# Folding the routing weight and 1+g2 into the experts' eviction, and rewriting the last phase of a two-layer decoder trunk

## The reference

```
expert, weight = top-1 group, top-2 experts in it        # per token: 2 experts, 2 weights
xbuf[dest]     = t[tok]                                  # tokens sorted by expert, 128 to a block
ybuf           = (silu(xbuf @ w_gate[e]) * (xbuf @ w_up[e])) @ w_down[e]
out[tok]      += ybuf[dest] * weight                     # two rows for each token
x              = layer_norm(ALPHA * x + (1 + g2) * out)
```

## Time and profile before

| | us |
|---|---|
| median of three runs (4647.74 to 4658.24) | 4656.67 |
| the profiled execution, its own time | 4658.7 |
| its span, first to last instruction | 4656.5 |
| route, layer 0: up to the store of the block table | 1312.3 |
| experts, layer 0: about | 1315 to 2032 |
| project("k") with Combine | 2032.6 to about 2414 |
| experts, layer 1: last store issued | 4466.4 |
| last phase, first issue to last instruction | 4470.1 to 4656.5 |

### The profile page before, as it was taken

One profiled execution on the slowest core, in us unless ns is written; L12 is line 12 of the kernel. 1 busy time (PEld: TensorE's weight loads), 2 busy tenths in 40 slices (PEclk: granted clock), 3 DMA queues, 4 the chain that ended last, 5 costly groups with the idle time before them and its releaser, 6 DMA issues. The chain is left out here.

```text
span 4656.5 us, 54505 instructions
## 1 busy us (share of the span) xinstructions
PE 3894.4 (84%) x17372; PEld 2848.0 (61%) x17372; DVE 2109.5 (45%) x4726; ACT 1530.3 (33%) x2925; POOL 686.2 (15%) x560
## 2 busy tenths in 40 slices
PE   6999795969779999958979979979957679999930
PEld 1788574858645555537767758868846545555510
DVE  5000215844445545546644332234349655455546
ACT  1222203623223333333321122245635323333322
POOL 0111000211100110114420003300013111011124
PEclk8999897979779999979989989989978679999965
DMA  8322312543179999965546532244444279999964
GB/s 290 113 94 77 122 60 88 180 147 105 65 250 382 383 383 381 383 228 170 177 130 200 170 118 78 65 128 127 148 145 137 71 271 382 383 382 383 382 215 176
DMA packets 637597, 950.82 MB, mean 204 GB/s; under 512 B 42309, under 2 KB 499925, under 8 KB 616213
## 3 DMA queue, kind: packets, MB, share of 16 engines
q1 hardware_dynamic: 587790, 775.23, 49.5%
q0 software_dynamic: 27360, 99.63, 5.8%
q10 hardware_dynamic: 22328, 74.48, 4.0%
HBM read 746.62 MB, written 202.62 MB: 204 GB/s over the span
## 5 line engine op out<-in xcount | busy, mean ns | idle before, releaser
L1416 PE MATMUL ex_gu<-ex_wgu,ex_hT 128*128 128x512 f32 x2016 | 918.3, 598 | 17.9 <-DMA ex_wgu<-in_moe_w_up_dram 10.9
L1416 PEld LDWEIGHTS ex_gu<-ex_wgu,ex_hT 128*128 128x128 f32 x2016 | 369.3, 191 | 416.4 <-issue 403.2
L1537 DVE TENSOR_TENSOR ex_wds<-ex_wd,ex_wds 128x2048 fp32r<-128x2048 f32 x126 | 288.8, 2292 | 251.8 <-ACT ex_wds L1476 251.8
L1435 PE MATMUL ex_acc<-ex_wds,ex_aT 128*128 128x512 f32 x1512 | 382.8, 402 | 6.1 <-DVE ex_aT L1533 6.1
L1950 PE MATMUL pvo_mm<-pvo_ws,pvo_hT 128*128 128x512 f32 x1536 | 357.4, 393 | 21.0 <-POOL pvo_hT L2101 19.4
L1950 PEld LDWEIGHTS pvo_mm<-pvo_ws,pvo_hT 128*128 128x128 f32 x1536 | 289.4, 189 | 82.9 <-POOL pvo_hT L2101 20.2
L938 PE MATMUL am_acc<-am_ws,am_yT 128*128 128x512 f32 x1152 | 310.8, 428 | 11.6 <-DVE am_yT L1059 8.6
L1435 PEld LDWEIGHTS ex_acc<-ex_wds,ex_aT 128*128 128x128 f32 x1512 | 277.1, 190 | 62.5 <-DVE ex_aT L1533 6.5
L1491 ACT ACTIVATE ex_sg<-ex_gu 128x256 f32<-128x256 f32 x126 | 48.3, 383 | 791.1 <-PE ex_gu L1416 791.1
L1950 PE MATMUL pk_mm<-pk_ws,pk_hT 128*128 128x512 f32 x1152 | 276.4, 398 | 29.4 <-DVE pk_part L2089 18.1
L1950 PE MATMUL pq_mm<-pq_ws,pq_hT 128*128 128x512 f32 x1152 | 270.8, 396 | 31.9 <-POOL pq_hT L2101 31.9
(11 more groups left out here) (327 smaller groups left out, 5671.5 us busy)
## 6 DMA issues: line engine op xcount, KB each, us to landing
ex_wgu<-in_moe_w_gate_dram SPq DMA_DIRECT2D x126, 1024.0 KB
ex_wgu<-in_moe_w_up_dram SPq DMA_DIRECT2D x126, 1024.0 KB
ex_wd<-in_moe_w_down_dram SPq DMA_DIRECT2D x126, 1024.0 KB, 10.4
ybuf_scratch<-ex_y ACTq DMA_DIRECT2D x126, 512.0 KB, 9.3
mod_w<-in_ada_w_dram SPq DMA_DIRECT2D x12, 2048.0 KB
pv_m_w<-in_ada_w_dram SPq DMA_DIRECT2D x16, 1536.0 KB, 7.4
vo_scratch<-pvo_vo SPq DMA_DIRECT2D x16, 1024.0 KB
x_scratch<-am_x SPq DMA_DIRECT2D x32, 512.0 KB, 3.4
```

What stands on the lines that cost most here:

```text
L1416: ins = nc.tensor.matmul(gu[j][:, :, :], hT[:, j, k, :], wgu[:, jw, k, :, :], start=(k == 0), stop=(k == KD - 1))
L1435: ins = nc.tensor.matmul(acc[half][:, :], aT[:, hi_a, k, :], wds[:, j, hi_w, k, half * CH:(half + 1) * CH], start=(k == 0 and n == 0), sto ...
L1537: nc.vector.tensor_tensor(wds[:, j, 1, :, :], wd[:, j, :, :], wds[:, j, 0, :, :], ALU.subtract).then_inc(wlo_ready, 1)
```

## The change

1. `route`: the one-hot tile `ohb` gets a second half that holds the weight in place of the token (one more DVE instruction for each of the 32 pairs), the product with PE has 128 columns in place of 64, and a table `slotw` of weights by slot is copied out and stored behind `slots`. `wt` is no longer stored.
2. `experts`: `slotw` and g2 are loaded at the start. DVE evicts both PSUM tiles with `scalar_tensor_tensor`, times the slot's weight and 1+g2. ACT copies the weight's column for each block after the SiLU, and no longer evicts.
3. `Combine`, now used in `project("k")` only: POOL adds the two gathered tiles, DVE adds ALPHA*x and takes the statistics, ACT takes the root, DVE normalises in two instructions. It loads three tensors in place of five, and `gather` runs one tile further ahead, behind `sum_experts` in POOL's list.
4. `combine`, the last phase, is written out by hand without loops: four tiles of buffers for the gathers and the loads, indices read in place, the sum of the two gathered tiles on DVE, the statistics on ACT with two summing passes, nothing on POOL but the gathers.

```diff
@@ route
-                    v.tensor_scalar(ohb[:, n, :], blk[:, :], blkf[:, c, j:j + 1], tokf[:, c:c + 1], ALU.is_equal, ALU.mult)
+                    v.tensor_scalar(ohb[:, n, 0, :], blk[:, :], blkf[:, c, j:j + 1], tokf[:, c:c + 1], ALU.is_equal, ALU.mult)
+                    v.tensor_scalar(ohb[:, n, 1, :], blk[:, :], blkf[:, c, j:j + 1], wt[:, c, j:j + 1], ALU.is_equal, ALU.mult)
                     v.tensor_scalar(ohr[:, n, :], rows[:, :], rowf[:, c, j:j + 1], None, ALU.is_equal).then_inc(hot_ready, 1)
...
+                v.tensor_copy(slotw[:, :], slot[:, 1, :]).then_inc(slot_ready, 1)
@@ experts
+                sp.dma_start(slotw[:, :], d["slotw"]).then_inc(w_in, 16)
+                sp.dma_start(gain[:, :], d["mod"][l:l + 1, 5 * D:6 * D].to_broadcast([P, D])).then_inc(c_in, 16)
...
+                def weight_column(b, j):
+                    act.wait_ge(y_dve, b)
+                    nc.scalar.activation(wcol[:, j, :], slotw[:, ds(b, 1)], ACT.Copy).then_inc(wcol_ready, 1)
...
                 def store(b, j):
-                    act.wait_ge(acc_ready, b + 2)
-                    act.wait_ge(stored[j], 8 * (b - j) + 16)
-                    nc.scalar.activation(y[:, j, CH:D], acc[1][:, :], ACT.Copy).then_inc(y_act, 1)
-                    act.wait_ge(y_act, b + 2)
                     act.wait_ge(y_dve, b + 2)
...
-                    nc.vector.tensor_copy(y[:, j, 0:CH], acc[0][:, :]).then_inc(y_dve, 1)
+                    dve.wait_ge(wcol_ready, b + 1)
+                    for half in range(2):
+                        cut = slice(half * CH, (half + 1) * CH)
+                        ins = nc.vector.scalar_tensor_tensor(y[:, j, cut], acc[half][:, :], wcol[:, j, :], gain[:, cut], ALU.mult, ALU.mult)
+                    ins.then_inc(y_dve, 1)
@@ Combine (now in project("k") only)
+        def sum_experts(c, j):
+            pool.wait_ge(self.y_in[j], 16 * (c - j) + 32)
+            nc.gpsimd.tensor_tensor(self.y[:, j, 0, :], self.y[:, j, 0, :], self.y[:, j, 1, :], ALU.add).then_inc(self.ysum_ready, 1)
+
+        return [(sum_experts, self.lead + 1), (gather, self.lead + 2)]
...
+        def total(c, j):
+            dve.wait_ge(self.x1_in[j], 8 * (c - j) + 16)
+            dve.wait_ge(self.ysum_ready, c + 1)
+            v.scalar_tensor_tensor(z[:, j, :], self.x1[:, j, :], ALPHA, self.y[:, j, 0, :], ALU.mult, ALU.add)
+            dve.drain().then_inc(self.y_used, 1)
...
         def normalise(c, j):
...
+            v.reciprocal(rstd[:, j, 2:3], rstd[:, j, 1:2])
+            v.scalar_tensor_tensor(z[:, j, :], z[:, j, :], mv[:, j, 0:1], norm[:, 0, :], ALU.subtract, ALU.mult)
             dve.drain()
+            v.scalar_tensor_tensor(self.x2[:, j, :], z[:, j, :], rstd[:, j, 2:3], norm[:, 1, :], ALU.mult, ALU.add).then_inc(self.x2_ready, 1)
+
+        return [(normalise, self.lead - 1), (total, self.lead)]
@@ combine (the last phase), RB = 4
+                def load(c, j):
+                    if c >= RB:
+                        sp.wait_ge(z_ready, c - RB + 1)
+                    sp.dma_start(x1[:, c % RB, :], d["x1"][c * P:(c + 1) * P, :]).then_inc(x1_in[c % RB], 16)
...
+                straight(sp, [(load, 3), (consts, 1), (store, -1)])
...
+                def gather(c, j):
+                    if c >= RB:
+                        pool.wait_ge(y_used, c - RB + 1)
+                    for n in range(2):
+                        nc.gpsimd.indirect_dma_start(out=y[:, c % RB, n, :], out_offset=None, in_=d["ybuf"],
+                                                     in_offset=bass.IndirectOffsetOnAxis(ap=dest[:, c, n:n + 1], axis=0)).then_inc(y_in[c % RB], 16)
...
+                def statistics(c, j):
+                    act.wait_ge(z_ready, c + 1)
+                    nc.scalar.activation(spare[:, :], z[:, j, :], ACT.Identity, accum_out=sums[:, j, 0:1])
+                    act.drain()
+                    nc.scalar.activation(sums[:, j, 1:2], sums[:, j, 0:1], ACT.Copy, scale=-1.0 / D)
+                    act.drain()
+                    nc.scalar.activation(spare[:, :], z[:, j, :], ACT.Square, bias=sums[:, j, 1:2], accum_out=sums[:, j, 2:3])
+                    act.drain()
+                    nc.scalar.activation(sums[:, j, 3:4], sums[:, j, 2:3], ACT.Sqrt, bias=eps[:, :], scale=1.0 / D).then_inc(std_ready, 1)
...
+                def total(c, j):
+                    dve.wait_ge(y_in[c % RB], 32 * (c // RB) + 32)
+                    v.tensor_tensor(z[:, j, :], y[:, c % RB, 0, :], y[:, c % RB, 1, :], ALU.add).then_inc(y_used, 1)
+                    dve.drain()
+                    dve.wait_ge(x1_in[c % RB], 16 * (c // RB) + 16)
+                    v.scalar_tensor_tensor(z[:, j, :], x1[:, c % RB, :], ALPHA, z[:, j, :], ALU.mult, ALU.add).then_inc(z_ready, 1)
...
+                def normalise(c, j):
+                    dve.wait_ge(std_ready, c + 1)
+                    v.reciprocal(rstd[:, j, :], sums[:, j, 3:4])
+                    v.scalar_tensor_tensor(z[:, j, :], z[:, j, :], sums[:, j, 1:2], norm[:, 0, :], ALU.add, ALU.mult)
+                    dve.drain()
+                    v.scalar_tensor_tensor(x2[:, j, :], z[:, j, :], rstd[:, j, :], norm[:, 1, :], ALU.mult, ALU.add).then_inc(x2_ready, 1)
+                    dve.drain()
+
+                straight(dve, [(total, 0), (normalise, -1)])
```

More of the change, by code:

```diff
@@ L1206, in _ @@
                     pe.wait_ge(hot_ready, n + 1)
-                    ins = nc.tensor.matmul(slot[:, :], ohr[:, n, :], ohb[:, n, :], start=(n == 0), stop=(n == 2 * NT - 1))
+                    ins = nc.tensor.matmul(slot[:, :, :], ohr[:, n, :], ohb[:, n, :, :], start=(n == 0), stop=(n == 2 * NT - 1))
                 ins.then_inc(slot_acc, 1)
@@ L1710, in pool_stages @@
-        return [(gamma, self.lead - 1), (gather, self.lead + 1)]
-    def scalar_stages(self, act):
-        nc, y, std = self.nc, self.y, self.std
-        def first_expert(c, j):
-            act.wait_ge(self.y_in[j], 16 * (c - j) + 32)
-            nc.scalar.activation(self.wb[:, j, :], self.wt[:, ds(c, 1), :], ACT.Copy)
-            act.drain()
-            nc.scalar.activation(y[:, j, 0, :], y[:, j, 0, :], ACT.Copy, scale=self.wb[:, j, 0:1]).then_inc(self.y0_ready, 1)
+        def sum_experts(c, j):
+            pool.wait_ge(self.y_in[j], 16 * (c - j) + 32)
+            nc.gpsimd.tensor_tensor(self.y[:, j, 0, :], self.y[:, j, 0, :], self.y[:, j, 1, :], ALU.add).then_inc(self.ysum_ready, 1)
@@ L1776, in combine, with straight @@
+def straight(eng, stages):
+    most, least = max(lead for _, lead in stages), min(lead for _, lead in stages)
+    for i in range(-most, NT - least):
+        for stage, lead in stages:
+            if 0 <= i + lead < NT:
+                stage(i + lead, (i + lead) % 2)
 def combine(nc, d, l):
+    RB = 4
     with Phase(nc, f"cb{l}") as ph:
-        cb = Combine(nc, d, l, ph)
+        norm = ph.sb("norm", [P, 2, D])
+        dest = ph.sb("dest", [P, NT, 2], I32)
+        x1 = ph.sb("x1", [P, RB, D])
+        y = ph.sb("y", [P, RB, 2, D])
+        z = ph.sb("z", [P, 2, D])
+        x2 = ph.sb("x2", [P, 2, D])
+        spare = ph.sb("spare", [P, D])
+        eps = ph.sb("eps", [P, 1])
+        sums = ph.sb("sums", [P, 2, 4])
+        rstd = ph.sb("rstd", [P, 2, 1])
+        dest_in, norm_in, eps_ready, y_used, z_ready, std_ready, x2_ready = (
+            ph.sem(s) for s in ("dest_in", "norm_in", "eps_ready", "y_used", "z_ready", "std_ready", "x2_ready"))
+        x1_in, stored = [ph.sem(f"x1_in{j}") for j in range(RB)], [ph.sem(f"stored{j}") for j in range(2)]
+        y_in = d["pool_dma"](f"cb{l}")
```

163 lines of the change are left out of this document (71 added, 92 removed).

## The result

The changed kernel takes **4540.3 us** (median of four runs, 4538.7 to 4551.6) against 4655.3 for the kernel before in the same comparison: ratio 0.976, 95% interval 0.974 to 0.978, 115 us less. I had forecast 4580 and a range from 4566 to 4612.

What follows compares the result with a forecast made beforehand. PE and DMA were taken to bound the experts, a chain the last phase, DVE route and PE project("k"). Last phase -79, route +14, experts +4, project("k") -17 sum to -78, giving 4580 us, range 4566 to 4612.

Steps and rivals of the forecast that it cites:

- Experts: Both experts phases: longer tail and the load of g2 cost 2.2 us each, +4 us in all.
- covered, if PE and DMA stay the bound: Experts' blocks: DVE's 0.7 us more a block hides in its idle 0.90 and 2.92 us.
- Last phase, pace: Last phase: DVE becomes the bound at 5.75 us a tile, 5.18 of instructions plus five gaps of 0.11; 92 us for 16.
- Last phase, ends: Last phase: first gather at 4472, first sum at 4479.5, end at 4577.6 against 4656.5; with the pace, -79 us.
- The drain: Last phase: a drain, not queue depth, held POOL 5.08 us before the next gather; without it gathers run ahead.
- The rival of two gathers in flight: Last phase: at most two gathers in flight, 16 tiles take 120 us in place of 92; +28, 4608 us; 14%.
- ACT's statistics: Last phase: ACT needs 3.0 to 3.4 us a tile, a summing output at most 0.2 each, under DVE's 5.75.
- The rival of switching tables: Last phase: ACT switches tables in every tile, 5.8 us a tile, level with DVE; +4, 4584 us; 3%.
- Route: Both route phases: 32 more DVE instructions, 6.5 us, plus 0.6 for a copy and an issue; twice, +14 us.
- DVE's eviction: Experts: DVE evicts two halves at 0.69 us each in place of one copy of 0.68; last eviction 1.4 us.
- The slower rival: Experts: DVE's evictions become the bound; at 3 us each 189 us more, 4769 us; 2%.
- Project("k"): project("k"): shorter chain saves 13.5 us, a wait of 5.6 goes, 2 taken off for POOL's sum; -17 us, bounds -8 and -20.

Runs made afterwards that it cites:

- e7_depth2: The changed kernel with two tiles of gathered rows in the last phase in place of four; the phase takes 108.5 us, 3.6 more.
- e8_drain: The changed kernel with a GpSimd drain ahead of each pair of gathers in the last phase but the first; the phase takes 143.8 us, 38.9 more.

## Why the prediction was wrong, step by step

- **Experts: the step that failed** is "covered, if PE and DMA stay the bound" with "the same 11 us a block". I read two full resources and took the block's time as given. PE's 199.2 busy us of 200 were not PE at its own pace: a block that nothing delays takes 10.77 us, ten of the 52 in the middle of layer 0 took less than 10.8 even before, and the mean was 10.95. The DMA engines alone were the bound, and 2% of their rate would show in full.
- **Last phase, pace:** the bound was right, DVE, but its gaps were mis-sized. The five instructions are 5.16 us (5.18 forecast); the step is 5.26 and not 5.75. Only the three gaps with a drain cost something, 0.07 to 0.09 each (1.32 from L1839 to L1842), and at the two others an instruction begins 0.07 to 0.08 before the one ahead of it has ended, so all five make 0.1 us and not 0.55. I had read 0.11 a gap from a step in which DVE waited a lot. That is -8 us. By my 383 GB/s the DMA engines needed 5.5 a tile, and would have been the bound at this pace; they moved 398.
- **Last phase, ends:** the first sum starts 13.5 us behind the phase's first issue, not 9.4. I took the median landing of 5.6 from the old phase; the first pair needs 11.4 from its issue. It isn't the number of gathers: with four issued (e7_depth2) it needs 11.1, with two (e8_drain) 11.3. What is left are the loads of x1 and of the two constants beside it, 3 MB, which no run took away, so that cause is not shown. The later start gives back half of what the pace brings, and -79 against -81.5 is partly luck.
- **The drain:** right, and shown by e8_drain, for what it does behind a gather; the pace of the old phase it didn't set. The rival of two gathers in flight fell with the first eight.
- **ACT's statistics:** right, 3.1 us a tile, a summing output costs 0.188 more. The rival of switching tables fell: one load in the phase, 1.28 us, with Identity, Square, Copy and Sqrt mixed. What a switch in every tile would cost is not shown, as none happened.
- **Route:** right, +7.8 a phase in the mean for +7.1.
- **DVE's eviction:** 0.743 us for a half and 1.40 for the pair, forecast 0.69 and 1.4; DVE's idle time before L1559 fell from 2.92 to 2.50 and it bounds nothing. The slower rival fell.
- **Project("k"):** PE's listed waits fell by 5.4, 12.2 and 0.6, and one for `pk_ws` rose by 1.4: 16.8 for 17. The phase fell by 21.1: the first matmul comes 7.0 us sooner in it (I had said about 9, and in the sum had taken off 2 for POOL's part), and the other 14.1 lie behind it. Some 3 of these don't show as waits, and I have no cause for them; the steady step, 19.6 to 19.8 us before, is 18.6 now. Of POOL's work I had counted all 6.1 us of a step as time that a normalise waits, and no run shows such a wait: L1744 is never stretched (1.268 in the mean), L1746 by 1.07 in the mean and by 1.43 at most. In the twelve tiles where the two meet a rotary sum, L1744 starts 0.09 to 0.10 us ahead of it and keeps its time, L1746 starts 1.24 to 1.25 behind its start and takes 2.70 to 2.71. That every normalise meets all of GpSimd's work was my assumption.
- **The range** was built from costs of the listed edits and had no room for a cause outside them.
